# Hybrid trunk kernel: the chunk inverse's last level on its 64x64 corner, parts of four weight pieces made anew, and a new step order

## The reference

```python
h = rmsnorm(x, pre_norm)
proj = jnp.einsum('bld,de->ble', h, w_in)            # columns of all groups
qkv = silu(causal_conv(concat([gq, gk, gv]), gdn_conv))
o_a = gated_deltanet(...)                            # 4 heads of 128
o_a = rmsnorm(o_a, gdn_norm) * silu(gz)
y_b = ssd(...) * silu(sz)                            # 16 heads of 64, 2 groups
o_b = rmsnorm(y_b by group, ssd_norm)
o_c = retention(rotary(rq), rotary(rk), rv)          # 4 heads of 128
o_c = rmsnorm(o_c, ret_norm) * silu(rg)
out = jnp.einsum('ble,ed->bld', concat([o_a, o_b, o_c]), w_out)
x = x + rmsnorm(out, post_norm)
```

```python
a_low = einsum('bihd,bjhd->bhij', k * beta, k) * decay * strict
sol = triangular_solve(a_low + eye, rhs, lower=True)  # rhs: v*beta and k*beta*exp(gcum)
v_new = u - w @ S
o = (q * exp(gcum)) @ S + attn @ v_new
S = S * exp(glast) + kdec.T @ v_new
```

## Time and profile before

| | |
|---|---|
| median of 3 runs | 2120.73 us (2119.14 to 2121.55) |
| profiled execution | 2119.12 us, its span 2117.3 us |
| granted clock of TensorE, mean | 0.991 |
| busy: TensorE, VectorE, ScalarE, POOL | 2044.3, 1416.7, 878.2, 482.3 us |
| moved by DMA | 410.59 MB, 194 GB/s |

### The profile page before, as it was taken

One profiled execution on the slowest core, in us unless ns is written; L12 is line 12 of the kernel. 1 busy time (PEld: TensorE's weight loads), 2 busy tenths in 40 slices (PEclk: granted clock), 3 DMA queues, 4 the chain that ended last, 5 costly groups with the idle time before them and its releaser, 6 DMA issues. The chain is left out here.

```text
span 2117.3 us, 38295 instructions
## 1 busy us (share of the span) xinstructions
PE 2044.3 (97%) x14628; PEld 1880.9 (89%) x14628; DVE 1416.7 (67%) x3428; ACT 878.2 (41%) x1771; POOL 482.3 (23%) x432
## 2 busy tenths in 40 slices
PE   7989999999999999999999999999999999999997
PEld 6768889999889998899888888889989899989997
DVE  5788866745578787623668887875466878575334
ACT  5544367423433236511444433754324433563011
POOL 3433343432000012100333333423300001120001
...
GB/s 244 247 179 152 204 173 210 239 212 305 189 170 161 138 207 189 163 166 146 185 262 198 199 194 154 299 191 252 239 206 214 133 170 139 178 270 130 159 106 184
DMA packets 98198, 410.59 MB, mean 194 GB/s; under 512 B 11169, under 2 KB 12257, under 8 KB 84193
## 3 DMA queue, kind: packets, MB, share of 16 engines
...
## 5 line engine op out<-in xcount | busy, mean ns | idle before, releaser
L1327 PE MATMUL ps<-w_hi,hT_hi 128*128 128x256 f32 x1792 | 524.3, 293 | 6.7 <-POOL w_low L2389 5.0
L1327 PE MATMUL ps<-w_hi,hT_lo 128*128 128x256 f32 x1792 | 503.4, 281 | 0.0
L1327 PE MATMUL ps<-w_low,hT_hi 128*128 128x256 f32 x1792 | 501.9, 280 | 0.0
L2389 POOL TENSOR_TENSOR w_low<-w_loaded,w_hi 128x512 fp32r<-128x512 f32 x208 | 283.5, 1381 | 429.0 <-ACT w_hi L2103 429.0
L1327 PEld LDWEIGHTS ps<-w_hi,hT_hi 128*128 128x128 f32 x1792 | 337.7, 188 | 13.7 <-POOL w_low L2389 6.3
L1327 PEld LDWEIGHTS ps<-w_low,hT_hi 128*128 128x128 f32 x1792 | 338.1, 189 | 4.4 <-issue 3.8
L1327 PEld LDWEIGHTS ps<-w_hi,hT_lo 128*128 128x128 f32 x1792 | 339.5, 189 | 0.0
L1327 PE MATMUL ps<-hT_hi,w_hi 128*128 128x512 f32 x768 | 319.5, 416 | 6.3 <-POOL w_low L2389 6.2
L1327 PE MATMUL ps<-hT_lo,w_hi 128*128 128x512 f32 x768 | 304.0, 396 | 0.0
L1327 PE MATMUL ps<-hT_hi,w_low 128*128 128x512 f32 x768 | 303.4, 395 | 0.0
L1327 PE MATMUL ps<-wo_parts,mixT_hi 128*128 128x256 f32 x960 | 270.0, 281 | 0.0
(11 more groups left out here) (215 smaller groups left out, 3792.6 us busy)
## 6 DMA issues: line engine op xcount, KB each, us to landing
w_loaded<-in_w_in SPq DMA_DIRECT2D x104, 512.0 KB, 5.0
...
w_hi<-w_split SPq DMA_DIRECT2D x104, 512.0 KB, 6.3
w_low<-w_split SPq DMA_DIRECT2D x104, 512.0 KB, 7.1
wo_loaded<-in_w_out SPq DMA_DIRECT2D x32, 512.0 KB, 4.2
wk<-cum_rows SPq DMA_DIRECT2D x32, 512.0 KB, 5.0
wo_split<-wo_parts SPq DMA_DIRECT2D x32, 512.0 KB, 8.5
```

The source lines that it names most:

```text
L1327: return nc.tensor.matmul(o, a, b, start=start, stop=stop)
L2389: tt(w_lo[at], wr[at], w_hi[at], ALU.subtract)\
```

## The change

1. **Last level.** `gdn_p` and `gdn_xx` of level 6 multiply only what isn't zero: 64 stationary columns (the second half of the matrix, the first half of PP) by 64 moving ones, into 64 partitions of a bank. VectorE copies that corner into PP without a mask and subtracts only the corner.
2. **Pieces 0 to 3.** `is_split` and `is_kept` replace the test for the first half: pieces 0 to 3 (`AGAIN`) aren't stored, and in the second half they are loaded as they are (1 MB) and split again by ScalarE and POOL. So a layer's second half has 16 `split` steps more.
3. **Order.** `PIECES` has another order, the planner other costs and constants. (`SPARE` is 0, so `slot_at` and `slot_owner` pick what was picked before.)

```diff
-PIECES = ([("gz", 0), ("gdn", 0), ("gdn", 1), ("gz", 1), ("bc", 0), ("gdn", 2), ("gdn", 3), ("bc", 1),
-           ("gdn", 4), ("sz", 0, 0), ("gdn", 5), ("sx", 0, 0), ("sx", 0, 1), ("sz", 0, 1), ("sx", 1, 0), ("sz", 1, 0),
+PIECES = ([("gz", 0), ("gdn", 0), ("gdn", 1), ("gz", 1), ("bc", 0), ("gdn", 2), ("bc", 1), ("gdn", 3),
+           ("sz", 0, 0), ("gdn", 4), ("sz", 0, 1), ("gdn", 5), ("sz", 1, 0), ("sx", 0, 0), ("sx", 0, 1), ("sx", 1, 0),
            ("sx", 1, 1), ("sz", 1, 1)]
+AGAIN = range(4)
             elif part == "sum":
-                mark("n", dve(900, *after))
+                mark("n", dve(1200, *after))
...
             elif part == "column":
-                mark("n", dve(len(cols) * 2 * (150 + 2 * BASE), *after))
+                mark("n", dve(len(cols) * 2 * (220 + 2 * BASE), *after))
...
-            mark("n", pe(2 * LINE))
-            mark(("pp", *step[1:]), dve(380, "n"))
+            mark("n", pe(2 * LINE if lv < LEVELS - 1 else LINE))
+            mark(("pp", *step[1:]), dve(380 if lv < LEVELS - 1 else 300, "n"))
...
-OUT_WAIT = 2500
-LATE = 200
+OUT_WAIT = 1000000000.0
+LATE = 500
-KEEP = 8
+KEEP = 2
-HOLD = 0
+HOLD = 500
-SLICE, LINE, TURN, UNIT, TABLE, MB, LANDING = 705, 224, 109, 24 * 119, 1283, 3500, 2300
+SLICE, LINE, TURN, UNIT, TABLE, MB, LANDING = 705, 224, 109, 24 * 119, 1283, 3300, 2000
+def is_split(n):
+    p, i = divmod(n, len(PIECES))
+    return p % 2 == 0 or i in AGAIN
+def is_kept(n):
+    p, i = divmod(n, len(PIECES))
+    return p % 2 == 0 and i not in AGAIN
 def kept_done(n):
-    return sum(32 for m in range(n % W_RING, n + 1, W_RING) if m // len(PIECES) % 2 == 0)
+    return sum(32 for m in range(n % W_RING, n + 1, W_RING) if is_kept(m))
@@ SP
-            if p % 2 == 0:
+            if is_kept(n):
                 loads.append((where["proj", p, i, 0, Q - 1], n, ("keep", p, i)))
...
-                        sp.wait_ge(w_kept[n % W_RING], kept_done(n - W_RING))
+                        if kept_done(n - W_RING):
+                            sp.wait_ge(w_kept[n % W_RING], kept_done(n - W_RING))
...
-                        if p % 2 == 0:
+                        if is_split(n):
                             sp.dma_start(wr[:, n % W_RING, cols], w_in[p // 2, key[2]][:, cols])
@@ TensorE, gdn_p and gdn_xx
-                        i = mm(b[:, c * P:(c + 1) * P], aTs[h % 2][:, 2 * j + c, :], X[:, 2 * j + c, :])
+                        if lv < LEVELS - 1:
+                            i = mm(b[:, c * P:(c + 1) * P], aTs[h % 2][:, 2 * j + c, :], X[:, 2 * j + c, :])
+                        else:
+                            i = mm(b[0:P // 2, c * P:c * P + P // 2], aTs[h % 2][:, 2 * j + c, P // 2:], X[:, 2 * j + c, 0:P // 2])
...
+                            i = mm(b[0:P // 2, c * P:c * P + P // 2], PP[:, 2 * j + c, 0:P // 2], XTs[h % 2][:, 2 * j + c, P // 2:])
@@ VectorE
-                        empty(tt(XT[:, own], XT[:, own], bank4(s)[:, 0:2], ALU.subtract), s)
+                        corner = XT[0:P // 2, own, P // 2:]
+                        empty(tt(corner, corner, bank4(s)[0:P // 2, 0:2, 0:P // 2], ALU.subtract), s)
...
-                    empty(tt(PP[:, own], bank4(s)[:, 0:2], over_rows(mask, 2), ALU.mult), s)
+                    if s[3] < LEVELS - 1:
+                        empty(tt(PP[:, own], bank4(s)[:, 0:2], over_rows(mask, 2), ALU.mult), s)
+                    else:
+                        empty(nc.vector.tensor_copy(PP[P // 2:, own, 0:P // 2], bank4(s)[0:P // 2, 0:2, 0:P // 2]), s)
```

More of the change, by code:

```diff
@@ L66 @@
 SLOTS = 2
+SPARE = 0
 MIX_BANKS = (2, 3, 4, 5, 6)
@@ L215, in front_steps @@
                     j, odd = divmod(Q * half + q - SPLIT_FROM, 2)
-                    if 0 <= j < 4 and not odd and (p + (i == len(PIECES) - 1)) % 2 == 0 and (p, i) != (PARTS - 1, len(PIECES) - 1):
+                    if 0 <= j < 4 and not odd and len(PIECES) * p + i + 1 < PARTS * len(PIECES) and is_split(len(PIECES) * p + i + 1):
                         add(("split", *((p, i + 1) if i + 1 < len(PIECES) else (p + 1, 0)), j))
@@ L264, in load_piece @@
         for half in range(2):
-            at["w_in", n, half] = dma(MB if n // len(PIECES) % 2 else MB // 2, *after)
+            at["w_in", n, half] = dma(MB // 2 if is_split(n) else MB, *after)
     def loaded_after():
@@ L278, in needs @@
             kk = q if wide else 2 * q % KD
-            out = [("w_in", n, kk // 4) if p % 2 else ("w_lo", n, kk // 2)] if half == 0 else []
+            out = [("w_lo", n, kk // 2) if is_split(n) else ("w_in", n, kk // 4)] if half == 0 else []
             if q == 0:
@@ L495, in play @@
             h, lv, j = r
-            mark("n", pe(2 * LINE))
-            mark(("x", p, h, lv + 1, j) if lv < LEVELS - 1 else ("xt", p, h, LEVELS, j), dve(380, "n"))
+            mark("n", pe(2 * LINE if lv < LEVELS - 1 else LINE))
+            mark(("x", p, h, lv + 1, j) if lv < LEVELS - 1 else ("xt", p, h, LEVELS, j), dve(380 if lv < LEVELS - 1 else 300, "n"))
         elif k == "gdn_s":
@@ L805, in unit_split_no @@
     return u - GROUPS * UNITS * ((u // (GROUPS * UNITS) + 1) // 2)
+def is_split(n):
[4 more added lines that the diff above has]
+    return p % 2 == 0 and i not in AGAIN
 def split_no(n):
-    return n - len(PIECES) * ((n // len(PIECES) + 1) // 2)
+    return sum(is_split(m) for m in range(n))
 def loads_done(n):
-    return sum(32 if m // len(PIECES) % 2 else 16 for m in range(n % W_RING, n + 1, W_RING))
+    return sum(16 if is_split(m) else 32 for m in range(n % W_RING, n + 1, W_RING))
 def kept_done(n):
-    return sum(32 for m in range(n % W_RING, n + 1, W_RING) if m // len(PIECES) % 2 == 0)
+    return sum(32 for m in range(n % W_RING, n + 1, W_RING) if is_kept(m))
 def slot_of(p, i, half):
@@ L832, in slot_of, with slot_owner @@
     return None
+def slot_owner(n):
+    if n is None or n < SLOTS + SPARE:
+        return None
+    return n - SLOTS - SPARE if n < 2 * SLOTS + SPARE else n - SLOTS
 def slot_reader(n):
@@ L853, in frees @@
     n = slot_of(p, i, half)
-    if n is not None and n >= SLOTS:
-        need.append(slot_reader(n - SLOTS))
+    if slot_owner(n) is not None:
+        need.append(slot_reader(slot_owner(n)))
     g = gate_of(p, i)
@@ L1078, in over_cols, with slot_at @@
             return a.unsqueeze(2).broadcast_to([P, a.shape[1], m])
+        def slot_at(n):
+            if SLOTS <= n < SLOTS + SPARE:
+                return acc[:, 2 * (n - SLOTS):2 * (n - SLOTS) + 2, :].rearrange("p t d -> p (t d)")
+            return slot[:, n % SLOTS, :]
         def mtile(p, i, half):
@@ L1156, in slot_wait @@
         def slot_wait(eng, n):
-            if n is None or n < SLOTS:
+            if slot_owner(n) is None:
                 return
-            r = slot_reader(n - SLOTS)
+            r = slot_reader(slot_owner(n))
             if r[0] == "gdn_open":
@@ L1445, in _ @@
                     h = s[2]
-                    own = slot[:, (10 * p + h) % SLOTS, :]
+                    own = slot_at(10 * p + h)[:, :]
                     b = opened(s)
@@ L1490, in _ @@
                     for c in range(2):
-                        left, right = (XTs[h % 2], PP) if lv < LEVELS - 1 else (PP, XTs[h % 2])
-                        i = mm(b[:, c * P:(c + 1) * P], left[:, 2 * j + c, :], right[:, 2 * j + c, :])
+                        if lv < LEVELS - 1:
+                            i = mm(b[:, c * P:(c + 1) * P], XTs[h % 2][:, 2 * j + c, :], PP[:, 2 * j + c, :])
+                        else:
+                            i = mm(b[0:P // 2, c * P:c * P + P // 2], PP[:, 2 * j + c, 0:P // 2], XTs[h % 2][:, 2 * j + c, P // 2:])
                     close(i, s)
@@ L1734, in _ @@
                             dve.wait_ge(S["ret_sum"], m)
-                        own = slot[:, (10 * p + 6 + h) % SLOTS, half * 512:half * 512 + 512]
+                        own = slot_at(10 * p + 6 + h)[:, half * 512:half * 512 + 512]
                         b = bank(tag).rearrange("p (t q e n) -> p t q e n", t=2, q=2, e=2)
-                        ns = slot[:, (10 * p + 6 + h) % SLOTS, 0:1024].rearrange("p (t q e n) -> p t q e n", t=NT, q=2, e=2)
+                        ns = slot_at(10 * p + 6 + h)[:, 0:1024].rearrange("p (t q e n) -> p t q e n", t=NT, q=2, e=2)
                         r0 = own.rearrange("p (t q e n) -> p t q e n", t=2, q=2, e=2)
```

21 lines of the change are left out of this document (11 added, 10 removed).

## The result

The changed kernel takes 2135.53 us (median of 4 runs, 2133.51 to 2137.69); the kernel before takes 2119.93 in the same comparison (4 runs). The ratio is 1.0071, 95% interval [1.0059, 1.0083]: 15 us slower. Forecast were 2101 us and a range up to 2115. The profiled execution took 2137.69 us around a span of 2135.9.

What follows compares the result with a forecast made beforehand. TensorE, busy 2044.3 of 2117.3 us, was taken as the bound. The terms -12.1 + 1.7 - 2.5 - 1.0 - 6 = -19.9 us, from 2119.1 and with 1.6 for the median, gave 2101 us, range 2089 to 2115.

Steps and rivals of the forecast that it cites:

- Term 5: New step order: half the loss at 140 to 160 us comes back, -6 us; elsewhere 0, ends -5 and +8.
- Term 1: Last level on 64 columns: 224 TensorE passes each 54 ns shorter through a shorter load, -12.1 us.
- a pass gets no shorter: Rival at the last level: an fp32 pass has a fixed cost of some 110 ns, giving 2113 us; chance 0.05.
- Term 2: VectorE's shorter operations at the last level, covered by projections: taken as 0, far end -1 us.
- Term 3: Parts of pieces 0 to 3 made anew in the second half come late and make TensorE wait: +1.7 us.
- term 4: Lighter DMA: -2.5 us at the changes of half, -1.0 us at the load of piece 4 in the first layer.
- The slower rival: At both changes of half ScalarE sticks on the row tile with a weight part behind it: 2129 us; chance 0.03.
- The 0.92 for faster: Whole kernel: chance 0.92 of coming out faster by more than 0.2% (4.2 us).

Runs made afterwards that it cites:

- e2: Kernel before with only the new step order, 128 columns at the last level, pieces 0 to 3 stored and loaded as before: 2140.43 us, ratio 1.0094.
- e7: Changed kernel with an output unit and a unit split moved to other places at each change of half: 2129.91 us, ratio 1.0052.
- e8: Changed kernel with HOLD = 0 instead of 500, so output units stand between the ret_o steps in the tail: 2131.22 us, ratio 1.0055.
- e9: Changed kernel with output unit (p-1, 3, 3, 1) moved ahead of head 3's turn, for p = 1 and 3: 2137.56 us, ratio 1.0089.
- e12: Changed kernel with two projection steps moved into the stretch from 197 to 217 us that had none: 2136.04 us, ratio 1.0068.
- e3: Kernel before, in its order and with 128 columns, with only the remade parts of pieces 0 to 3 added: 2117.47 us, ratio 0.9989.
- e13: Kernel before plus remade parts, 96 columns in both last-level products, row tile 2's squares behind piece 0's last high part: 2113.25 us, ratio 0.9976.
- e14: Changed kernel with the edits of e7 and e8, 96 columns, and row tile 2's squares behind piece 0's last high part: 2111.80 us, ratio 0.9963.

## Why the prediction was wrong

- **Term 5, the new order, -6 us: the step that failed.** Measured alone it costs 20 us (e2). What it said of 140 to 160 us was right, and too cautious: 11.4 of the 13.2 us there went. "Elsewhere taken as 0, ends -5 and +8" was wrong: elsewhere the loss grew by 33 us in all. It compared how much TensorE work stands between two steps of a chain, at the median. That says nothing of the places where no projection stands at all, of the row tile's place in SyncE's queue, or of the ring of banks. In e2 the loss is 14.4 us more from (0, 11) to (0, 12), 5.0 more where mixing begins, 11.8 at the changes of half, 5.1 at head 3's turn, 6.1 in the tail and 5.8 in the first 18 pieces of layer 1. The first two are paid for by the gains beside them, so the net 20 us are the others. Two are shown by edits that take back a part (e7, e8). For head 3's turn (e9) and the bare stretch (e12) the edit tried cured nothing, and the 5.8 us weren't looked into. The bare stretch can be read from the step list before a run.
- **Term 1, -12.1 us.** The load of 64 columns is shorter (136 ns by its group, as forecast) and passes inside a group are 58 ns apart, as forecast. But the sum took a pass's price to be its load alone. The way in (94 ns) and out (94 and some 50 to 100 ns of the next pass) cost more than four shorter passes save (216): +5.0 us of intervals, 0 to +3 of time. The Trainium skill ("TensorE: Matmul & The Clock Gate", section "Back-to-back issue gap") states for 1 to 64 moving columns an issue floor of about 25 ns, and about 62 ns per matmul as the bound only with hardware decode off. At the 58 ns measured, the 62 did not bind. The rival "a pass gets no shorter" had about the right size (0 us) for the wrong reason.
- **Term 2** (VectorE, 0) can't be told from noise. **Term 3** (+1.7) and **term 4** (-3.5): together right in the old order (e3: -2.3), for mixed reasons. Less traffic did not bring the row tile sooner (9.6 us from issue to use, against a hoped 7.1), and term 4 looked only at the weight pieces around the tile in SyncE's queue, not at the load of an output unit ahead of it, where SyncE stood for 8.4 us; the far end "+4 for a landing of 9 us at both" was the nearer one: e3 loses 1.8 us more at the changes of half. The gain came from the first 135 us, 4.6 us against the 1.0 that the piece 4 load was given, in one trace each.
- **The slower rival** (ScalarE stuck on the row tile with a weight part behind it, 0.03) is real: TensorE waits 3.75 and 6.6 us for exactly that part. But it is worth 2 to 3 us (e13, e14), the queue ahead of the tile more, and its chance of 0.03 was too small because it was priced as the only way to lose. The 0.92 for faster rested on the order costing at most 8 us anywhere else: without term 1 the sum still stood at -7.8.
